# TensorE's multiplications of constants are taken out at the norms and at the router

## What is computed

```python
# first_block, two layers
x = x + _retention(_rmsnorm(x, ret_norm), ret_w_in, ret_w_out)
x = x + _conv_ffn(_rmsnorm(x, ffn_norm[0]), ...)
x = x + _stick_breaking(_rmsnorm(x, sb_norm), sb_w_in, sb_w_out)
x = x + _conv_ffn(_rmsnorm(x, ffn_norm[1]), ...)
x = _rmsnorm(x, final_norm)
# second_block, one layer
hn = rms_norm(x, g_norm1) * (1.0 + scale1) + shift1      # the modulated norm
x = x + gate1 * (concat(mlstm(hn), moba(hn)) @ w_out)
hn2 = rms_norm(x, g_norm2) * (1.0 + scale2) + shift2     # the norm ahead of the router
x = x + gate2 * hierarchical_moe(hn2, ...)               # 32 experts, top 2 inside a top group
return rms_norm(x, g_final)
```

## Time and profile before

| | |
|---|---|
| three runs | 1386.33, 1388.24, 1388.9 us; median 1388.24 |
| the profiled execution | 1385.47 us, of which the profiled span is 1383.8 us |
| TensorE busy | 1343.1 us of the span, 97% |
| VectorE busy | 739.1 us, 53% |
| ScalarE busy | 558.9 us, 40% |
| TensorE's mean granted clock | 0.996 |

### The profile page before, as it was taken

One profiled execution on the slowest core, in us unless ns is written; L12 is line 12 of the kernel. 1 busy time (PEld: TensorE's weight loads), 2 busy tenths in 40 slices (PEclk: granted clock), 3 DMA queues, 4 the chain that ended last, 5 costly groups with the idle time before them and its releaser, 6 DMA issues.

```text
span 1383.8 us, 19741 instructions
## 1 busy us (share of the span) xinstructions
PE 1343.1 (97%) x8020; PEld 980.5 (71%) x8020; DVE 739.1 (53%) x1299; ACT 558.9 (40%) x855; POOL 33.4 (2%) x54
## 2 busy tenths in 40 slices
PE   8999899999999999999999999989999999999996
PEld 8988578888878898899988787764544454445442
DVE  5754556877756544698875777862222222222222
ACT  4434545555555377565554655521111111111111
POOL 2000000111100000000000000000000000000000
PEclk9999999999999999999999999999999999999999
DMA  9557353989953553255655463388999999999994
GB/s 339 194 200 259 107 166 126 313 293 309 359 181 125 180 184 122 71 183 182 243 187 196 155 243 122 122 365 352 429 426 428 427 430 428 429 428 429 428 429 188
DMA packets 112723, 372.73 MB, mean 269 GB/s; under 512 B 4476, under 2 KB 64156, under 8 KB 99984
## 3 DMA queue, kind: packets, MB, share of 16 engines
q1 hardware_dynamic: 104784, 344.07, 64.5%
q0 software_dynamic: 7872, 27.76, 5.8%
HBM read 370.75 MB, written 1.05 MB: 269 GB/s over the span
## 4 chain that ended last, share of the span: by engine, by line
PE 83%; DMA 7%; DVE 6%; ACT 3%; issue 1%; DVEq 0%; SPq 0%; ACTq 0%
PE ps L637 14%; PE ps L1473 13%; PE ps L599 8%; PE ps L600 8%; PE ps L601 8%; PE ps L1494 7%; PE ps L1456 4%; PE ps L614 3%; PE ps L615 3%; PE ps L616 3%; DMA ring<-in_w_expert_up_dram 3%; DMA arena<-in_w_expert_up_dram 3%; DVE w_low L536 2%; PE ps L1059 2%; PE ps L1500 2%; DMA ring<-in_ret_w_in_dram 1%
## 5 line engine op out<-in xcount | busy, mean ns | idle before, releaser
L536 DVE TENSOR_TENSOR w_low<-ring,w_high 128x1024 fp32r<-128x1024 f32 x264 | 311.4, 1221 | 160.3 <-ACT w_high L528 160.3
L528 ACT ACTIVATE w_high<-ring 128x1024 fp32r<-128x1024 f32 x264 | 264.9, 1052 | 213.4 <-PE ps L637 90.2
L599 PE MATMUL ps<-h_high,w_high 128*128 128x256 f32 x1088 | 312.6, 287 | 3.7 <-DVE w_low L536 2.3
L600 PE MATMUL ps<-h_low,w_high 128*128 128x256 f32 x1088 | 307.7, 283 | 0.0
L601 PE MATMUL ps<-h_high,w_low 128*128 128x256 f32 x1088 | 307.6, 283 | 0.0
L599 PEld LDWEIGHTS ps<-h_high,w_high 128*128 128x128 f32 x1088 | 208.3, 191 | 23.6 <-DVE arena L2035 12.6
L600 PEld LDWEIGHTS ps<-h_low,w_high 128*128 128x128 f32 x1088 | 208.6, 192 | 0.0
L601 PEld LDWEIGHTS ps<-h_high,w_low 128*128 128x128 f32 x1088 | 208.4, 192 | 0.0
L1473 PE MATMUL ps<-ring,arena 128*64 128x512 f32 x608 | 176.6, 594 | 2.2 <-DMA arena<-in_w_expert_gate_dram 1.2
L1473 PEld LDWEIGHTS ps<-ring,arena 128*64 128x64 f32 x608 | 57.4, 137 | 110.9 <-issue 110.8
L637 PE MATMUL ps<-w_high,h_high 128*128 128x512 f32 x304 | 95.1, 394 | 4.7 <-DVE h_low L552 3.0
(11 more groups left out here) (361 smaller groups left out, 1655.6 us busy)
## 6 DMA issues: line engine op xcount, KB each, us to landing
ring<-in_ffn_w_up_dram SPq DMA_DIRECT2D x44, 1024.0 KB, 7.7
ring<-in_w_expert_up_dram SPq DMA_DIRECT2D x20, 2048.0 KB, 22.1
ring<-in_w_expert_down_dram SPq DMA_DIRECT2D x18, 2048.0 KB, 25.7
ring<-in_w_expert_gate_dram SPq DMA_DIRECT2D x18, 2048.0 KB, 23.3
ring<-in_ret_w_in_dram SPq DMA_DIRECT2D x11, 2048.0 KB, 8.0
arena<-in_w_expert_gate_dram SPq DMA_DIRECT2D x11, 2048.0 KB, 27.1
ring<-in_ffn_w_down_dram SPq DMA_DIRECT2D x10, 2048.0 KB, 7.9
arena<-in_w_expert_down_dram SPq DMA_DIRECT2D x9, 2048.0 KB, 23.2
```

The source lines that it names most:

```text
L528: nc.scalar.activation(hi, raw, ACT.Copy).then_inc(hi_done, 1)
L536: last = eng.tensor_tensor(lo, raw, hi.bitcast(F32), ALU.subtract)
L599: nc.tensor.matmul(o, hi, hTh[:, k, :], start=(k == 0), stop=False)
L600: nc.tensor.matmul(o, hi, hTl[:, k, :], start=False, stop=False)
```

## The change

`idle_turns` is kept, and so is its call ahead of the first rows. The other calls go, with the arguments that only served them. The call in `late_pe` had a count of 0.

```diff
         def late_pe(pe, r, turns=0):
             for t in range(NT):
-                if t:
-                    idle_turns(turns, 4, P)
                 for j in range(4):
...
-        def norm_pe(pe, r, turns=0):
+        def norm_pe(pe, r):
             n = N_TR[r]
-            idle_turns(turns)
             pe.wait_ge(norm_xn, LATE + NT * (n - LATE + 1))
...
                     if t == NT - 1:
                         last.then_inc(norm_tr, 1)
-                if t == 0:
-                    idle_turns(3, 4, T)
...
             late_pe(pe, 1)
-            idle_turns(3, 4, T)
             pe.wait_ge(ada_c, 1)
             ffn(0)
...
             late_pe(pe, 3)
-            idle_turns(3, 4, T)
             ffn(1)
-            norm_pe(pe, 5, 10)
+            norm_pe(pe, 5)
...
             nc.tensor.matmul(ps[:, 5, 128:128 + NE], ones, asg[:, 1, :], start=False, stop=True).then_inc(t_lg, 1)
-            idle_turns(3, 6, T)
```

## The result

| | us |
|---|---|
| before, 15 runs | 1387.68 median (1384.79 to 1389.17) |
| after the change, 15 runs | 1391.85 median (1390.14 to 1393.42) |
| ratio after to before | 1.0029, 95% interval 1.0022 to 1.0037 |
| profiled execution after | 1392.64, span 1390.8 |

The change makes the kernel 4.2 us slower. The forecast was +4.0 us, or 1392.2 us, counted from the median of three runs.

The account below looks back on a forecast made before the run. TensorE's chain, then the experts' weight stream, was taken to bound the kernel. −0.2 + 3.6 + 0 + 0.6 = +4.0 us on the 1388.24 us median gave 1392.2 us, range 1388.5 to 1396.5 for 8 in 10.

Parts of the forecast that it names:

- What bounds the kernel: Whole kernel: TensorE's chain, then the experts' weight stream; delay before the first refill at 938.5 moves the end.
- FFN norms: Two FFN norms: turned blocks start about 0.1 us earlier at each, no clock fall; −0.2 us.
- Modulated norm: 9.4 us wait there: clock falls, turned blocks lose 1.4 us and gate columns 2.2; +3.6 us.
- the two cases: Start and router in the trace: clock returns after 5.8 or 3.3 us of work, bounding the gate columns' loss.
- The other end of the range: Modulated norm: clock is back when the gate columns (L1233) start, so only the turned blocks pay, +1.4 us.
- Norm ahead of the router: Two tiles ahead of the router: TensorE waits for tile 1 anyway; 0 us.
- the first rival: Norm ahead of the router: clock falls over the logits' 32 passes, +2 to +3 us, 1394 to 1396; chance 0.13.
- Router: Router's gather: starts 0.7 us earlier but runs partly at the lower clock; +0.6 us, between −1.4 and +1.3.
- The rival of turned blocks: Modulated and FFN norms: turned blocks don't count as clock work, 6.4 us on top, 1398.6; chance 0.02.
- The rival of a faster kernel: Router and first gate: most executions before lose 2.8 us to spells the earlier gather escapes; 1384 us, chance 0.04.

Follow-up runs that it names:

- e10: e9's version with only the ten idle turns at the modulated norm taken out; 1385.91 us, 0.9991 of the kernel before.
- e13: The same version as e10, run once more; 1387.73 us, 1.0002 of the kernel before.
- e6: Kernel before with only the three idle turns between the two tiles ahead of the router taken out; 1387.12 us, ratio 1.0000.
- e7: Kernel before with only the router's three idle turns behind the ranks taken out; 1388.40 us, ratio 1.0007.
- e9: e4's version plus five idle turns behind the ranks and turns in the last expert pair's waits; 1385.35 us, 0.9982 of the kernel before.
- e2: Changed kernel with the ten idle turns at the modulated norm put back; 1388.62 us, 1.0004 of the kernel before.
- e11: Kernel before with six instead of ten idle turns at the modulated norm, placed late in the wait; 1388.05 us, ratio 1.0010.
- e3: Kernel before with the router's three idle turns behind the ranks out and five put ahead of the wait for VectorE's choice of experts; 1387.00 us, ratio 1.0001.
- e4: e3's version without idle turns at the FFN norms, with turns filling TensorE's waits at the retention's end; 1387.68 us, 1.0002 of the kernel before.
- e1: Kernel before with only the ten idle turns at the modulated norm taken out; 1392.07 us, ratio 1.0032.
- e12: The same version as e9, run once more; 1385.24 us, 0.9983 of the kernel before.

## Why the prediction was right, by its own steps

- **What bounds the kernel.** Right. Idle turns at the norm only fill a wait; the turned blocks start 9.25 us after the last product, as before. Delay ahead of the first refill reaches the end nearly in full: 7.13 us there, 7.00 at the end.
- **FFN norms, −0.2 us.** Measured −0.03 in the profile: the first product of the first FFN comes as late behind its turned blocks as before (3.32 us), so nothing was won. Nothing fell there. The reason given, that the retention stands more at the higher level, rested on one execution: six of nine profiles of the same code fall there.
- **Modulated norm, +3.6 us.** Right in mechanism and size: +3.50 in the profile (turned blocks and what waits for them +1.67 where 1.4 was worked out, gate columns +1.83 where 2.2 was), +3.9 us on the median with this edit alone. Counting the return of the clock from the gate columns rather than from the turned blocks gave the right number for the profiled executions: it came 3.7 us behind their start. The reason for that choice, the wait of 1.2 us between the two, is not shown. Counted from the first turned block TensorE was busy for 7.5 us before the clock was back, more than either of the two cases (3.3 and 5.8 us) allows, so these bounds were no bounds for work as such. The other end of the range, 1.4 us, may be what some of the runs of e10 and e13 paid.
- **Norm ahead of the router, 0.** In the profile the first rival happened, +1.09 us instead of +2 to +3. The rival priced all 32 passes at the lower level; the spell began 1.5 us into them and they lost 1.9 us, and VectorE's normed copy of `x`, which stood in the chain before, hid 0.7 to 0.8 of it. The sum had put this place at nothing. On the median no cost of it shows (e6).
- **Router, +0.6 us.** +0.40 in the profile (0.5 us won by the earlier start, gather 5.47 instead of 4.54 us from its first instruction), +1.7 in e7's, where the range ended at +1.3. Right in mechanism, and in size for the changed kernel.
- **The rival of turned blocks.** The Trainium skill ("TensorE: Matmul & The Clock Gate", Part 4, "PE-mode transpose") says that a transpose doesn't count as TensorE being busy in the same way. The rival took from this that the clock would fall at the FFN norms. It did not: with the turns there out, e9's profile is at 1.00 from 8.8 to 1374 us, over both, and none of the six other profiles without them has a spell there. The prediction's own evidence against the rule was weak, though. The retention's turned blocks and waits kept 1.00 in the profile before and had a spell in six of nine. That, and the late return at the modulated norm, would fit blocks that count for less; no run tests it.
- **The rival of a faster kernel** rested on spells before that the profile does not show. They exist in some executions, in the retention, where the change does not touch them; at the router the changed kernel and e7 fall as well.

Luck had a part. The places other than the norm come to +0.5 us together on the median in e2, where +0.4 was forecast, but part by part they were +1.1 instead of 0 and +0.4 instead of +0.6 in the profile. The norm's sum came within 0.1 us because two misses cancel, 0.3 us too little for the turned blocks and 0.4 too much for the gate columns. And a sum made against the after profile alone would have called the change 7 us.

## What to carry to other kernels

Where TensorE waits for a chain on other engines, look for what the clock does behind the wait: a wait of 9 us cost 3.5 us there, dummy products that end 5 us before the wait did saved nothing, and about as many in its last part saved most of it. Neither the busy share nor the idle stretch told alone whether the clock falls: it stood 3.25 us of idling in e11 and fell in e3 with 3.61 of 4.70 us busy. Check every wait of the program in more than one profile, since with the retention filled the clock still fell at the router and at the last pair (e4), and the median did not move. Before a difference of a few microseconds is put down to an edit, compare the places that the edit does not touch: here 2.2 us of 7.0 came from one of them.

## What was not expected of the hardware

- The clock can fall in a stretch with a good deal of work: 3.61 us busy of 4.70 (e3), and then stay at the lower level for 6.6 us, 6.03 of them busy; in the profile before it was back after 3.3. In the retention the same code kept 1.00 in some executions and had a spell of 6.8 us in others.
- A spell can begin when the work is already back: after the change, the logits were under way (919.1), and e1's spell at the last pair began in the down products (1370.0).
- The rise at the start moves too. The thirty idle turns at the start begin at 2.87 us in the profile before and take 6.36 us; in e3's they begin at 2.78 and take 5.00, with the passes of 421 ns giving way to those of 275 about 3 us sooner. So the prediction's 5.8 us of work before the return was one execution's value.
- The runs of one kernel lie 4 us and more apart, and the slower ones have the lower mean clock: of the thirty of before beside e1, those up to 1386 us have 0.995 to 0.997, those from 1389 us on 0.992 or 0.993. Filling the waits lifts the clock more surely than it narrows the runs: 0.995 to 0.997 against 0.991 to 0.997, within 2.8 us against 3.7 (e9); 0.995 to 0.998 against 0.992 to 0.996, within 3.2 us against 3.1 (e12).
